# Where two weight pieces are rounded and split: in the attention by pairs, or in the memory steps behind it

## The chip, the cores and the metric

The kernel runs as one program on one core of a Trainium2 chip. The metric is the device time of one execution in microseconds. TensorE (PE) multiplies, VectorE (DVE) and ScalarE (ACT) work on its results, GpSimd (POOL) does a few side jobs, and SyncE (SP) issues the weight transfers.

## What is computed

The reference is two models in a row on 256 tokens of width 1024. The second one, "the second block" here, has two layers. Each of its layers mixes tokens with a windowed attention and a chunkwise matrix memory (an mLSTM), puts both results through one output projection, and then runs a feed-forward part (in the last layer a mixture of experts). Cut to what the change touches:

```
def merge_groups(att, h_ml, o_pre, g_att, g_ml, w_out):
    att_n = rmsnorm(att, g_att)
    hn = hf * lax.rsqrt(jnp.mean(hf * hf, axis=-1, keepdims=True) + EPS)      # hf: the memory's heads
    ml = hn.reshape(B, T, ML_WIDTH) * jax.nn.sigmoid(o_pre)
    return jnp.concatenate([att_n, ml], axis=-1) @ w_out

out_x = merge_groups(att_x, h_xf + flip(h_xb), om_x, g_att, g_ml, w_out)
out_c = merge_groups(att_c, h_cf + flip(h_cb), om_c, g_att, g_ml, w_out)      # first layer only
```

## The kernel before, in words

**Products of three.** A float32 product is made of three products in a rounded format. A weight piece of 128x2048 comes by DMA into a slot of `ring` (six slots). ScalarE rounds it into one of three slots of `ring_hi` (`weights_hi`, the copy at L1551), and VectorE subtracts the rounded part from the piece, in place (`weights_lo`, L2216, which writes `ring_r`). TensorE then reads both. `hi_upto(n)` and `lo_upto(n)` do the next roundings or subtractions until n pieces are done; `first_split["out0"]` and `first_split["out1"]` are the numbers of the first pieces of the two output projections, which have four pieces each. Because the engines run their instructions in the written order, the place of such a call in the code is its place in the engine's queue.

**Attention by pairs** (`attend_pairs(l)`, one for each engine, l is the layer, 0 or 1). A "half" is a pair of heads and 128 queries. There are 16 halves in the first layer (8 over 4x128 keys, 8 over 2x128 keys) and 8 in the last. For half n TensorE makes the scores, VectorE takes their maximum (L2281, L2283), ScalarE takes the exponential (L1630), TensorE turns it (L785), and VectorE and ScalarE each copy one head's turned part out of PSUM (into `pair_pT`, named `extra` in the profile). After every second half TensorE multiplies with the values, and VectorE evacuates that (L2304 to L2311). In this loop stand, in the kernel before, the roundings of pieces 0 and 1 (after n = 2 and 3, ScalarE) and their subtractions (after n = 3 and 5, VectorE).

**Memory steps.** They follow at once. A step n is one chunk, one memory head and one direction: 16 in the first layer, 8 in the last. A step's number n below is the loop index of this part. TensorE makes the row maximum and scores of step n+2 (`row_max`, L466) and then the step's product with the values, into bank 6 or 7 by turns (the rows with outputs of 128x129: 14 matmuls in the steps with four tiles). VectorE makes the exponents of step n+1 (L2785), the weights of step n (`weights`, L2801, which the product of step n waits for), and after each second step the scaled output of two steps (`heads_out`, L2816 to L2821). ScalarE makes the exponentials of step n+1 (L2000, L2002), which the weights of step n+1 wait for, and the magnitude of the step's denominator (L2033), and sums of squares (L2007, L2016). In the first layer, after step 4, ScalarE also takes a square root between two table loads (L1590, L1579). The bank of step n's product is free for step n+2 only when `heads_out` has read it.

**Output projection.** The heads are scaled and turned, rounded and split like the weights, and multiplied with the four pieces. Pieces 2 and 3 are rounded and split in this part, in both kernels.

Of the kernel before, what the change touches and what calls it, by code (L numbers as in the profile page):

```python
# [209 lines left out]
def build(nc, A, out):  # L210
    ctx = ExitStack()
    with ctx:
# [148 lines left out]
        first_split = {}  # L361
# [1185 lines left out]
        def _(act):  # L1547
# [64 lines left out]
            def attend_pairs(l):  # L1612
# [10 lines left out]
                for n, w in enumerate(hv):  # L1623
                    L.wait("pair_m", 16 * l + n + 1)
                    for hd in range(2):
                        if n >= 2:

                            look(act, "pair", l, "pT", n - 2, hd)
                        u, i = look(act, "pair", l, "s", n, hd), 2 * n + hd
                        leave(act.activation(pair_p[:, 2 * (n % 2) + hd, 0:w.keys * P], ps[:, u.bank, 0:w.keys * P],  # L1630
                                             ACT.Exp, bias=pair_neg[:, i:i + 1], scale=AD ** -0.5,
                                             accum_out=pair_den[:, i:i + 1]), u)
                    if n % 2:
                        j = n // 2
                        L.wait("pair_sink", 8 * l + j + 1)
                        v = pair_sink[:, 4 * j:4 * j + 4]
                        L.send(act.activation(v, v, ACT.Exp), "pair_esink")
                    if n:
                        copy_pT(n - 1)
                    if n in (2, 3):  # L1640
                        hi_upto(first_split[f"out{l}"] + n - 1)
                copy_pT(len(hv) - 1)

            def weights_hi(j):
# [299 lines left out]
            for l in range(2):  # L1944
# [81 lines left out]
                for n, (sq, x, d) in enumerate(steps):  # L2026
# [13 lines left out]
                        preload(ACT.Exp)  # L2040
                    if l == 0 and n in (6, 7):
                        mix_att((2 * n - 12, 2 * n - 11))
                    if l == 0 and n in MIX_AT:
                        mixT_hi(l, [MIX_AT.index(n)])
                    if n >= 2 and n % 2 == 0:
# [63 lines left out]
            with act.Fori(0, n_passes) as i:  # L2109
# [10 lines left out]
                for p, (e, c) in enumerate(EXPERT_ORDER):  # L2120
# [16 lines left out]
                    n = e * NP + c // 2  # L2137
# [15 lines left out]
        def _(dve):  # L2153
# [119 lines left out]
            def attend_pairs(l):  # L2273
# [47 lines left out]
                for n in range(len(hv)):  # L2321
# [4 lines left out]
                        heads(n // 2 - 1)  # L2326
                    if n >= 2 and n % 2 == 1:
                        output(n // 2 - 1)
                    if n in (3, 5):
                        lo_upto(first_split[f"out{l}"] + n // 2)  # L2330
                heads(len(hv) // 2 - 1)
                output(len(hv) // 2 - 1)

# [360 lines left out]
            for l in range(2):  # L2694
# [134 lines left out]
                for n in range(len(steps)):  # L2829
# [5 lines left out]
                    if l == 0 and n == 5:  # L2835
                        inverted("merge_rstd", 1, stat[:, 16:20])
                        dve.sem_inc(sig("merge_ready"), 1)
                    if l == 0 and n - 1 in MIX_AT:
                        mixT(l, [MIX_AT.index(n - 1)])
                heads_out(len(steps) // 2 - 1)  # L2840
# [271 lines left out]
```

## Time and profile before

| what | us |
|---|---|
| median of three runs | 2487.19 |
| lowest and highest | 2484.7, 2491.62 |
| the profiled execution | 2489.2 |
| its span, first to last instruction | 2487.4 |
| first layer: attention by pairs, then memory steps | about 885 to 937, then to 1008 |
| last layer: attention by pairs, then memory steps | about 1542 to 1578, then to 1617 |

The page has one line for each engine (busy time and share of the span), the span in 40 slices, the chain of work that ended last, and groups of instructions. TensorE is busy for 97% of the span, VectorE 68%, ScalarE 50%. The share of the whole span says nothing on the two places of the change, which together are about 160 us long; these are read from the rows in order of time. In such a row an idle time before an instruction stands in brackets, with what ended it; an idle time that is too short is left out, and rows that follow each other may overlap by what the pipeline overlaps.

### The profile page before, as it was taken

The numbers are of one execution on the slowest core, as the hardware profiler recorded it, in microseconds if no ns is written. First come the engines' busy times: TensorE is split into PE (matmuls) and PEld (weight loads), VectorE is DVE, ScalarE is ACT, GpSimd is POOL, SyncE is SP. The second block draws the span as 40 slices with busy tenths as digits, with TensorE's granted clock in tenths as the row PEclk, the third lists the DMA queues.
The fourth block names the chain that finished last, engine by engine and source line by source line (L and its number), as shares of the span: only waits on it lengthen the run. The fifth ranks groups of instructions, "written<-read, shape, count | busy, mean of one in ns | idle before, by whom it ended". The sixth has DMA issues, their size and how long they took to land.

```text
span 2487.4 us, 35121 instructions
## 1 busy us (share of the span) xinstructions
PE 2407.0 (97%) x13490; PEld 2008.3 (81%) x13514; DVE 1685.7 (68%) x1931; ACT 1233.3 (50%) x1471; POOL 436.4 (18%) x359
## 2 busy tenths in 40 slices
PE   8999999999999998899999999889999999999998
PEld 6669998879998866678888887578888888888887
DVE  7555864466854766467655348658888888888887
ACT  5454334444333354332222144447777777777775
POOL 1003541004520000010003500003122131121221
PEclk9999999999999998899999989989999999999999
DMA  6564554414552310135555332028989989989895
GB/s 237 213 244 163 187 187 148 150 60 154 186 196 87 105 43 1 48 121 188 201 196 185 127 107 97 1 88 313 369 333 353 357 333 363 347 339 370 332 363 208
DMA packets 71605, 503.59 MB, mean 202 GB/s; under 512 B 8208, under 2 KB 8720, under 8 KB 11536
## 3 DMA queue, kind: packets, MB, share of 16 engines
q1 hardware_dynamic: 70272, 496.68, 54.6%
q0 software_dynamic: 1168, 4.66, 0.5%
q8 instruction: 109, 1.79, 0.3%
q14 instruction: 56, 0.46, 0.1%
HBM read 500.26 MB, written 1.05 MB: 202 GB/s over the span
## 4 chain that ended last, share of the span: by engine, by line
PE 89%; DVE 5%; ACT 3%; issue 1%; POOL 1%; DMA 0%; SPq 0%; DVEq 0%; ACTq 0%
PE ps L466 85%; PE ps L530 1%; DVE h L2189 1%; POOL h_r L1433 1%; PE ps L1252 1%; DVE ring_r L2216 1%; DVE h_r L2183 1%; PE ps L785 1%; DVE temp L2281 0%; PE ps L634 0%; ACT ring_hi L1551 0%; DMA cols<-in_cols 0%; DVE temp L2552 0%; ACT h L1599 0%; DVE h L2801 0%
## 5 line engine op out<-in xcount | busy, mean ns | idle before, releaser
L1551 ACT ACTIVATE ring_hi<-ring 128x2048 fp32r<-128x2048 f32 x427 | 807.1, 1892 | 566.6 <-PE ps L466 345.4
L2988 DVE TENSOR_TENSOR ring_r<-ring,ring_hi 128x2048 fp32r<-128x2048 f32 x264 | 617.6, 2346 | 121.0 <-ACT ring_hi L1551 119.1
L466 PE MATMUL ps<-ring_hi,extra_r 128*128 128x512 f32 (+2 forms) x1808 | 607.9, 392 | 6.9 <-DVE ring_r L2216 4.8
L2216 DVE TENSOR_TENSOR ring_r<-ring,ring_hi 128x2048 fp32r<-128x2048 f32 (+3 forms) x163 | 380.3, 2340 | 180.2 <-ACT ring_hi L1551 166.2
L466 PE MATMUL ps<-extra_r,ring_hi 128*128 128x256 f32 (+1 forms) x1432 | 461.1, 322 | 8.4 <-DVE ring_r L2216 4.6
L466 PE MATMUL ps<-extra_r,ring_r 128*128 128x256 f32 (+1 forms) x1432 | 457.5, 319 | 0.0
L466 PE MATMUL ps<-h_r,ring_hi 128*128 128x256 f32 (+2 forms) x1400 | 445.1, 318 | 0.0
L466 PE MATMUL ps<-ring_r,extra_r 128*128 128x512 f32 (+2 forms) x1104 | 422.7, 383 | 0.0
L466 PEld LDWEIGHTS ps<-ring_hi,extra_r 128*128 128x128 f32 x1808 | 341.3, 189 | 80.5 <-DVE ring_r L2216 6.0
L466 PEld LDWEIGHTS ps<-extra_r,ring_hi 128*128 128x128 f32 x1432 | 273.4, 191 | 32.4 <-DVE ring_r L2216 5.2
L466 PEld LDWEIGHTS ps<-extra_r,ring_r 128*128 128x128 f32 x1432 | 273.3, 191 | 19.0
L466 PEld LDWEIGHTS ps<-h_r,ring_hi 128*128 128x128 f32 (+1 forms) x1400 | 267.6, 191 | 17.6
L466 PEld LDWEIGHTS ps<-ring_r,extra_r 128*128 128x128 f32 x1104 | 208.8, 189 | 37.9 <-issue 0.2
L1491 POOL TENSOR_TENSOR areaA_r<-areaA,ones 128x256 fp32r<-128x256 f32 x88 | 111.0, 1261 | 607.6 <-ACT areaA L2093 607.6
L466 PE MATMUL ps<-ring_hi,h_r 128*128 128x512 f32 (+2 forms) x400 | 147.2, 368 | 0.0
L466 PE MATMUL ps<-areaA_r,ring_hi 128*128 128x256 f32 (+1 forms) x736 | 140.8, 290 | 0.0
L466 PE MATMUL ps<-ring_hi,areaB_r 128*128 128x512 f32 x352 | 139.8, 397 | 0.0
L466 PE MATMUL ps<-ring_r,areaA_r 128*128 128x512 f32 x352 | 138.0, 392 | 0.0
L466 PE MATMUL ps<-ring_hi,areaA_r 128*128 128x512 f32 x352 | 137.7, 391 | 0.0
L466 PEld LDWEIGHTS ps<-areaA_r,ring_hi 128*128 128x128 f32 x736 | 117.0, 194 | 1.2
L1453 POOL TENSOR_TENSOR areaA_r<-areaB,areaA_r 128x256 fp32r<-128x256 f32 x44 | 115.8, 2633 | 3.5
L2552 DVE CUSTOM_DVE_ANT_0 temp<-ring,areaB 128x1024 f32<-128x1024 f32 x80 | 105.6, 1320 | 6.1 <-DVE areaA L2892 4.3
(372 smaller groups left out, 3014.0 us busy)
## 6 DMA issues: line engine op xcount, KB each, us to landing
ring<-in_experts SPq DMA_DIRECT2D x264, 1024.0 KB, 4.9
ring<-in_stream SPq DMA_DIRECT2D x202, 1024.0 KB, 4.9
ring<-in_stream SPq DMA_DIRECT2D x6, 512.0 KB, 3.7
ring<-in_stream SPq DMA_DIRECT2D x2, 576.0 KB, 3.6
res<-in_xT SPq DMA_DIRECT2D x2, 512.0 KB, 4.1
res<-in_ctxT POOLq DMA_DIRECT2D x1, 1024.0 KB, 7.3
h<-in_consts POOLq DMA_DIRECT2D x2, 512.0 KB, 5.1
areaB<-in_cond_rows POOLq DMA_DIRECT2D x1, 1024.0 KB, 6.3
```

The costliest lines, as they stand in the source:

```text
L466: return pe.matmul(o, l, r, start=start, stop=stop, skip_group_check=True)
L530: pe.matmul(ps[:, u.bank, :], warm_l, warm_r, start=True, stop=True, skip_group_check=True)
L785: m = pe.transpose(ps[:, u.bank, k * P:(k + 1) * P], pair_p[:, 2 * (n % 2) + hd, k * P:(k + 1) * P], ident)
L1252: m = pe.transpose(ps[:, 3, s * P:(s + 1) * P], mprod[:, n % 2, s * P:(s + 1) * P], ident)
L1433: pool.tensor_tensor(h_lo[:, hf, k, :], h[:, hf, k, :], h_hi[:, hf, k, :].bitcast(F32), ALU.subtract).then_inc(sig("h_lo"), 1)
L1453: pool.tensor_tensor(lo, src, hi.bitcast(F32), ALU.subtract).then_inc(sig("hidden_ready"), 1)
L1491: pool.tensor_tensor(hi, mturn[:, n % 2, :], ones[:, 0:1].broadcast_to([P, NM]), ALU.mult).then_inc(sig("moe_hi"), 1)
L1551: return act.activation(dst, src, ACT.Copy)
L2183: L.send(STT(out=h_lo[:, hf, k, :], in0=h[:, hf, k, :], scalar=shift(hf, k), in1=h_hi[:, hf, k, :].bitcast(F32), op0=ALU.add, op1=ALU.subt ...
L2216: L.send(TTN(ring_lo[:, s, 0:n], ring[:, s, 0:n], ring_hi[:, j % HIS, 0:n].bitcast(F32), ALU.subtract), "weights_lo")
L2552: S(dve.tensor_tensor_reduce(out=temp[:, :], in0=chunk[1][:, a * D:(a + 1) * D], in1=cond_rows[:, x, :], scale=1.0, scalar=0.0, op0=ALU.mu ...
L2988: TTN(ring_lo[:, s, :], ring[:, s, :], ring_hi[:, j % HIS, :].bitcast(F32), ALU.subtract).then_inc(sig("weights_lo"), 1)
```

## The change

The roundings of pieces 0 and 1 leave ScalarE's attention loop and stand in its memory loop: piece 0 in step 2, piece 1 in step 4, behind the sum of squares or the square root and ahead of L2016. The subtractions leave VectorE's attention loop and stand in its memory loop behind `heads_out`: piece 0 in step 4, piece 1 in step 6. This holds for both layers. The instructions themselves, their number, and the order on TensorE, GpSimd and SyncE stay as they are.

```diff
--- before.py
+++ after.py
@@ -1637,8 +1637,6 @@
                         L.send(act.activation(v, v, ACT.Exp), "pair_esink")
                     if n:
                         copy_pT(n - 1)
-                    if n in (2, 3):
-                        hi_upto(first_split[f"out{l}"] + n - 1)
                 copy_pT(len(hv) - 1)
 
             def weights_hi(j):
@@ -2040,6 +2038,8 @@
                         preload(ACT.Exp)
                     if l == 0 and n in (6, 7):
                         mix_att((2 * n - 12, 2 * n - 11))
+                    if n in (2, 4):
+                        hi_upto(first_split[f"out{l}"] + n // 2)
                     if l == 0 and n in MIX_AT:
                         mixT_hi(l, [MIX_AT.index(n)])
                     if n >= 2 and n % 2 == 0:
@@ -2326,8 +2326,6 @@
                         heads(n // 2 - 1)
                     if n >= 2 and n % 2 == 1:
                         output(n // 2 - 1)
-                    if n in (3, 5):
-                        lo_upto(first_split[f"out{l}"] + n // 2)
                 heads(len(hv) // 2 - 1)
                 output(len(hv) // 2 - 1)
 
@@ -2835,6 +2833,8 @@
                     if l == 0 and n == 5:
                         inverted("merge_rstd", 1, stat[:, 16:20])
                         dve.sem_inc(sig("merge_ready"), 1)
+                    if n in (4, 6):
+                        lo_upto(first_split[f"out{l}"] + n // 2 - 1)
                     if l == 0 and n - 1 in MIX_AT:
                         mixT(l, [MIX_AT.index(n - 1)])
                 heads_out(len(steps) // 2 - 1)
```

The line numbers of the kernel after are two lower from this loop on (L2016 is L2014 there, L2801 is L2799).

ScalarE in step 2 of the first layer, before: the denominator, two sums of squares, and the exponentials of step 4.

```order
L2033 ACTIVATE stat<-ps 128x2
L2007 ACTIVATE temp,stat<-areaA 128x512
L2016 ACTIVATE temp,stat<-areaA 128x128 x2
L2000 ACTIVATE h<-ps,temp 128x256 x2
L2002 ACTIVATE h<-h 128x512
```

After:

```order
L2031 ACTIVATE stat<-ps 128x2
L2005 ACTIVATE temp,stat<-areaA 128x512
L1551 ACTIVATE ring_hi<-ring 128x2048
L2014 ACTIVATE temp,stat<-areaA 128x128 x2
L1998 ACTIVATE h<-ps,temp 128x256 x2
L2000 ACTIVATE h<-h 128x512
```

One `ring_hi` instruction now stands between the first and the second sum of squares, ahead of the exponentials. Step 4 has the same, behind its last table load.

VectorE in step 4 of the first layer, before: `heads_out`, then the exponents of step 6 and the weights of step 5.

```order
L2816 TENSOR_TENSOR stat<-stat,temp 128x4
L2817 RECIPROCAL stat<-stat 128x4
L2819 TENSOR_TENSOR areaA<-ps,stat 128x2x128
L2821 SCALAR_TENSOR_TENSOR areaA<-ps,stat,areaA 128x128 x2
L2785 SCALAR_TENSOR_TENSOR h<-ps,temp,h 128x256 x2
L2801 SCALAR_TENSOR_TENSOR areaB<-ps,areaB 128x512 x2
```

After:

```order
L2814 TENSOR_TENSOR stat<-stat,temp 128x4
L2815 RECIPROCAL stat<-stat 128x4
L2817 TENSOR_TENSOR areaA<-ps,stat 128x2x128
L2819 SCALAR_TENSOR_TENSOR areaA<-ps,stat,areaA 128x128 x2
L2216 TENSOR_TENSOR ring_r<-ring,ring_hi 128x2048
L2783 SCALAR_TENSOR_TENSOR h<-ps,temp,h 128x256 x2
L2799 SCALAR_TENSOR_TENSOR areaB<-ps,areaB 128x512 x2
```

One `ring_r` instruction now stands ahead of those exponents and weights. Step 6 has the same.

VectorE behind half 3 of the first layer's attention, before: the maximum of half 5, an output, and the copy of half 4's turned part.

```order
L2281 TENSOR_REDUCE temp<-ps 128x2
L2283 SCALAR_TENSOR_TENSOR temp<-temp,rows 128x2
L2288 TENSOR_TENSOR temp<-temp,rows 128x4
L2311 TENSOR_TENSOR areaA<-ps,temp 128x2x128
L2216 TENSOR_TENSOR ring_r<-ring,ring_hi 128x2048
L2158 COPY extra<-ps 128x4x128
```

After:

```order
L2281 TENSOR_REDUCE temp<-ps 128x2
L2283 SCALAR_TENSOR_TENSOR temp<-temp,rows 128x2
L2288 TENSOR_TENSOR temp<-temp,rows 128x4
L2311 TENSOR_TENSOR areaA<-ps,temp 128x2x128
L2158 COPY extra<-ps 128x4x128
```

The subtraction ahead of the copy (`extra`) is gone; half 5 had the same.

## Rows read from the trace of the kernel before

**Rows 1.** The page: span, and the chain that ended last, by engine.

```profile
span 2487.4 us, 35121 instructions
...
PE 89%; DVE 5%; ACT 3%; issue 1%; POOL 1%; DMA 0%; SPq 0%; DVEq 0%; ACTq 0%
```

**Rows 2.** TensorE in order of time, first layer's attention: start, us, operation [idle <-releaser].

```profile
909.50 1.09 PE L785 MATMUL ps<-cst,h 128*128 128x128 f32 x8 [0.25 <-DVE extra L2158]
...
917.22 1.09 PE L785 MATMUL ps<-cst,h 128*128 128x128 f32 x8 [1.25 <-DVE extra L2158]
```

**Rows 3.** TensorE in order of time, last layer's attention.

```profile
1565.34 1.09 PE L785 MATMUL ps<-cst,h 128*128 128x128 f32 x8 [0.25 <-DVE extra L2158]
...
1573.06 1.09 PE L785 MATMUL ps<-cst,h 128*128 128x128 f32 x8 [1.89 <-DVE extra L2158]
```

**Rows 4.** VectorE in order of time, first layer's attention.

```profile
914.28 2.28 DVE L2216 TENSOR_TENSOR ring_r<-ring,ring_hi 128x2048 fp32r<-128x2048 f32 x1
916.48 0.68 DVE L2158 COPY extra<-ps 128x512 f32<-128x512 f32 x1
```

**Rows 5.** ScalarE in order of time, first layer's attention.

```profile
897.46 1.92 ACT L1551 ACTIVATE ring_hi<-ring 128x2048 fp32r<-128x2048 f32 x1
899.26 0.69 ACT L1630 ACTIVATE h<-ps,temp 128x512 f32<-128x512 f32 x1
```

**Rows 6.** Chain that ended last, first layer's memory steps: start, us, what.

```profile
959.34 0.69 ACT temp L2016 x4
...
961.31 1.29 DVE h L2801 x2
...
967.14 1.28 ACT L1579
...
970.72 1.29 DVE h L2801 x2
```

**Rows 7.** VectorE in order of time, first layer's memory steps.

```profile
964.68 1.28 DVE L2801 SCALAR_TENSOR_TENSOR areaB<-ps,areaB 128x512 f32<-128x512 f32 x2
...
974.10 1.28 DVE L2801 SCALAR_TENSOR_TENSOR areaB<-ps,areaB 128x512 f32<-128x512 f32 x2
```

**Rows 8.** TensorE in order of time, first layer's memory steps.

```profile
966.11 1.80 PE L466 MATMUL ps<-areaA,areaB 128*128 128x129 f32 x14 [0.26 <-DVE areaB L2801]
...
972.81 2.91 PE L466 MATMUL ps<-areaA,h 128*128 128x129 f32 x14 [1.38 <-DVE areaA L2819]
...
976.79 3.38 PE L466 MATMUL ps<-areaA,areaB 128*128 128x129 f32 x14
```

**Rows 9.** TensorE in order of time, last layer's memory steps.

```profile
1606.46 1.83 PE L466 MATMUL ps<-areaA,areaB 128*128 128x129 f32 x14
1610.06 1.83 PE L466 MATMUL ps<-areaA,h 128*128 128x129 f32 x14 [1.78 <-DVE areaA L2819]
1612.00 1.80 PE L466 MATMUL ps<-areaA,areaB 128*128 128x129 f32 x14
```

**Rows 10.** VectorE in order of time, last layer's memory steps.

```profile
1601.29 1.29 DVE L2801 SCALAR_TENSOR_TENSOR h<-ps,h 128x512 f32<-128x512 f32 x2 [0.54 <-ACT h L2002]
...
1604.97 1.28 DVE L2801 SCALAR_TENSOR_TENSOR areaB<-ps,areaB 128x512 f32<-128x512 f32 x2
```

**Rows 11.** Chain that ended last, last layer, behind the last memory step.

```profile
1614.24 0.18 ACT stat L2033
```

**Rows 12.** Busy us in stretches; the number after PEclk: is the granted clock's share.

```profile
core 0: us, PE busy (x) PEld busy (x) DVE busy (x) ACT busy (x) POOL busy (x), PEclk, DMA share, GB/s
976.00:980.00 4.00, 4.00 (x16) 3.22 (x15) 1.57 (x3) 2.24 (x7) 0.00 (x0) 0.50 0.02 4
1604.00:1608.00 4.00, 4.00 (x30) 3.47 (x30) 2.97 (x7) 2.00 (x8) 0.00 (x0) 1.00 0.00 0
```

**Rows 13.** TensorE in order of time, last layer, ahead of the first memory step.

```profile
1577.72 1.99 PE L466 MATMUL ps<-areaB 64*128 64x256 f32 x8
...
1580.70 3.59 PE L466 MATMUL ps<-areaB 64*128 64x256 f32 x8
```

## The prediction

> **What bounds the kernel now.** I read the page first: the span, and the chain that ended last by engine [rows 1]. 89% of that chain is TensorE, but the change leaves TensorE's own order alone, so the question is where TensorE waits. I therefore read TensorE in order of time at the two places of the change, and then the engine that is named in each bracket.
>
> In the attention by pairs TensorE is nearly always at work. Its idle times that have to do with the moved work are four: 0.25 and 1.25 us in the first layer [rows 2], 0.25 and 1.89 us in the last [rows 3]. Each ends with a copy into `extra` on VectorE, and that copy stands right behind a `ring_r` subtraction of 2.28 us, 2.20 us from start to start [rows 4]. The two roundings on ScalarE cost 1.80 us each from start to start [rows 5]; no idle time of TensorE follows them, because TensorE still has a half's scores or a product with the values to do.
>
> In the memory steps it is different. There the chain that ended last itself goes through ScalarE and VectorE: sums of squares of ScalarE in step 2, then (through exponentials) the weights of step 4 on VectorE at 961.31, and in step 4 the table load at 967.14, the same instructions again, and the weights of step 6 at 970.72 [rows 6]. The new place of piece 0's rounding is right ahead of the row at 959.34, that of piece 1's right behind the row at 967.14. Both are on the chain.
>
> **What is removed.** No instruction goes; four roundings and four subtractions (two of each per layer) change place. I take all four idle times as gained, since the copy that ends each moves forward by 2.20 us, more than any of them: 0.25 + 1.25 = 1.5 us in the first layer and 0.25 + 1.89 = 2.1 us in the last. Together 3.6 us. What is late next is TensorE itself. For the roundings that leave I count nothing. The bounds of this term are 0 (if another copy ends the same idle time) and 3.6; I stand by 3.6, because the rows show nothing else between the two instructions.
>
> **What is added, first layer.** Rounding piece 0: ScalarE's exponentials of step 4 come 1.80 us later, and the weights of step 4, which wait for them, too: 961.31 becomes 963.1. Everything behind is later by 1.80, as TensorE's product of step 4 waits for VectorE there. Rounding piece 1 is put between the table load and the sums, behind that product: another 1.80. The weights of step 6 go from 970.72 to 974.3, later by 3.6 us.
>
> Subtracting piece 0 (VectorE, step 4) adds 2.20 us ahead of the weights of step 5: from 964.68 [rows 7] to 964.68 + 1.80 + 2.20 = 968.7, so that TensorE's product of step 5 goes from 966.11 [rows 8] to about 970.0. It is over at 971.8. The weights of step 6 wait for ScalarE until 974.3 anyway, so this subtraction lies in the shadow of ScalarE and costs nothing of its own. If ScalarE's 3.6 us weren't there, it would cost up to 2.2.
>
> Subtracting piece 1 (VectorE, step 6) has no such cover. From the weights of step 6 to those of step 7 VectorE works without a break, 974.10 - 970.72 = 3.38 us [rows 6, 7]. With the subtraction it is 3.38 + 2.20 = 5.58 us, and the weights of step 7 run from 974.3 + 5.58 = 979.9 to 981.2. TensorE's product of step 7, which began at 976.79 [rows 8], begins at 981.2: later by 4.4 us. Of the 5.8 us by which the weights are late, 1.4 are absorbed by TensorE's own work between. Behind step 7 TensorE works through, so 4.4 us stay.
>
> **What is added, last layer.** The same with fewer covers. The weights of step 4 go from 1601.29 [rows 10] to 1603.1. From there to the weights of step 5 I take the 3.38 us of unbroken work plus 2.20: 1608.7 instead of 1604.97. They take 1.28, so TensorE's product of step 5 goes from 1606.46 [rows 9] to 1610.0, later by 3.5: here no square root hides the subtraction. The rounding of piece 1 on ScalarE runs beside it and is hidden. The product takes 1.83 us, to 1611.8; then ScalarE's magnitude and 1.4 us of `heads_out` to 1613.4, then the second subtraction to 1615.6, then the weights of step 7 to 1616.9, and TensorE's last product begins at 1617.0 instead of 1612.00 [rows 9]: 5.0 us. Before, the magnitude behind that product started at 1614.24 [rows 11], 0.4 us after the product's end, held by a table load; that slack is used up, and 4.6 us remain.
>
> Both additions have bounds. The lowest is 0, if the idle time of ScalarE and VectorE hid all; the highest is four roundings of 1.80 and four subtractions of 2.20, 16.0 us. The sum 4.4 + 4.6 = 9.0 us lies between and is worked out wait by wait, so I take it.
>
> **The clock.** In the first layer's memory steps the granted clock was 0.50 (1.2 GHz) from 976 to 980; in the last layer's it was 1.00 (2.4 GHz) from 1604 to 1608 [rows 12]. The fall in the first layer came behind 1.38 us of waiting, and the product of 14 matmuls then took 2.91 and 3.38 us in place of 1.83 [rows 8, 9]. The change puts waits of 1 to 2.4 us into both. In the first layer the product of step 7 is at the low level already, and could also meet the high one: 1.6 us to be lost or won. In the last layer that product would be 3.38 - 1.83 = 1.6 us longer if the clock has fallen by then. I take half of that, 0.8 us, as it lies between its two rows, and keep -1.6 and +5.4 (both layers, below) as the ends of the term.
>
> The Trainium skill, "TensorE: Matmul & The Clock Gate", section "HAM oscillation — how this bites in real kernels", says that gaps in a loop of matmuls throttle the clock again and that the penalty is paid at each return. By that rule the last layer's steps would lose the full level surely. The row of the first layer agrees with it; none of before shows it in the last layer. With the rule taken as certain the sum would be about 2 us higher; the sum here goes without it.
>
> **The sum.** -3.6 + 9.0 + 0.8 = +6.2 us. The profiled execution took 2489.2 us, so the same execution changed would take 2495.4. It was 2.0 above the median of 2487.2; against the median I predict 2493.4 us, 0.25% slower. About 0.3%, 7.5 us, is what a measurement can tell from no change, so "no change" here reaches up to 2494.7.
>
> **The rivals.**
> The clock falls in the last layer and comes back later in the first; this ends on the other side, slower by over 0.3%. For: the new waits, and the fall after 1.38 us [rows 8]. Against: in the last layer TensorE's product of step 6 waited 1.78 us and still took 1.83 us, and that of step 7 1.80 [rows 9]. Place: TensorE from step 5 on. Price: in the last layer the products of steps 5 and 7 are 1.1 (2.91 against 1.83) and 1.6 us longer, 2.7 in all, and I take the same again for the first layer, where two products behind step 7 would meet the low level. It decides once the clock takes 2.1 us (7.5 less 5.4). -3.6 + 9.0 + 2.7 + 2.7 = +10.8: 2498.0.
>
> The clock holds longer at the end of the attention. Ahead of the first memory step eight matmuls took 1.99 us at the high level and, a moment later, 3.59 at the low one [rows 13]. With the 1.89 us gone the fall might come later, or not at all: 1.6 us for these, as much again for what follows, some 3.5. Against: the first layer had only 1.25 us to wait, long before, and its clock fell there all the same. +5.4 - 3.5 + 0.8 = +2.7: 2489.9.
>
> The moved work hides. VectorE has idle time in the steps (0.54 us ahead of the weights of step 4, [rows 10]), and so has ScalarE; if the new instructions fall into such time, only the 3.6 us of gain are left: 2483.6, still within 0.3%. Against: the chain goes through just these places [rows 6]. With the clock held in both layers as well (another 7 us) it would be 2476.6, the one case that is faster by over 0.3%.
>
> **How the numbers follow.** My forecast (both effects, small clock term) 0.50; the clock falls 0.26; the clock holds 0.12; hidden 0.08; hidden and held 0.04. The forecast's own range, with a median that may lie 2 us off, is 2489 to 2497; 0.12 of its 0.50 lies above 2494.7. Slower by over 0.3% is then 0.26 + 0.12 = 0.38, within 0.3% is 0.38 + 0.12 + 0.08 = 0.58, faster 0.04. The range that leaves out 2 in 10 goes from 2487.5 (half of the hidden cases and some of the held below) to 2499.5 (the dearest of the clock cases above).
>
> **What would show it.** In the profile of the changed kernel: in the attention the idle times of 1.25 and 1.89 us before L785 are gone. The weights of step 4 begin some 1.8 us later than before, counted from the first product of the steps, those of step 6 by 3.6 in the first layer, and TensorE's product of step 7 by 4.4 and 5.0. New idle times of TensorE stand ahead of the products of steps 4 and 5, ended by VectorE. The attention of both layers is 1.5 and 2.1 us shorter, the memory steps some 4.5 longer each. The forecast is wrong if TensorE's new waits in the memory steps sum to less than the 3.6 us gained, or if the granted clock in the stretch between the attention's end and the first memory step is 1.00.

## The result, and the profile after

The kernel after took 2500.04 us, the median of 7 runs (2492.07 to 2505.79), beside 2487.19 for the kernel before (7 runs, 2484.7 to 2491.62). The ratio of the two is 1.0041, with an interval of 1.0029 to 1.0052; on 2487.2 that is 2497.4 us (2494.4 to 2500.1), slower by 10.2 us or 0.41%; the interval's lower end is 0.29%. Forecast were 2493.4 us and no change that can be told. The time is that of the first rival (2498.0), which had a chance of 0.26. The median of these seven runs lies 0.5 us above the range's upper end of 2499.5; what the ratio gives lies inside.

The runs of the kernel after spread over 14 us, those before over 7. The profiled execution is the fastest of the seven, 2492.07 us, and its span is only 2.9 us above that of before, so its trace holds less than a third of the loss. Its page, the line that answers to [rows 1]:

```profile
span 2490.3 us, 35145 instructions
```

TensorE in order of time, the first layer's attention and then the last layer's: the two places in each layer where before an idle time stood. The columns are those of [rows 2, 3].

```profile
909.26 1.09 PE L785 MATMUL ps<-cst,h 128*128 128x128 f32 x8
...
915.58 1.09 PE L785 MATMUL ps<-cst,h 128*128 128x128 f32 x8
```

```profile
1563.52 1.09 PE L785 MATMUL ps<-cst,h 128*128 128x128 f32 x8
...
1569.22 1.40 PE L785 MATMUL ps<-cst,h 128*128 128x128 f32 x8
```

No bracket is left in these rows: the idle times of 0.25, 1.25, 0.25 and 1.89 us that ended with `extra` are gone, all four, as forecast. One that wasn't forecast has come, 0.48 us ahead of the first layer's last turned half (931.95), ended by `extra` too.

The chain that ended last, first layer's memory steps, kernel after; it answers to [rows 6].

```profile
955.78 0.05 ACT ring_hi L1551
...
957.48 0.68 ACT temp L2014 x4
...
959.43 1.29 DVE h L2799 x2
...
961.03 0.43 DVE areaA L2817
...
961.51 3.39 PE ps L466 x14
...
964.93 0.17 ACT stat L2031
...
968.62 0.02 ACT ring_hi L1551
...
970.44 0.68 ACT temp L2014 x4
...
975.06 2.20 DVE ring_r L2216
```

Both roundings now stand on this chain (the rows at 955.78 and 968.62; ScalarE's next one starts 1.7 and 1.8 us later), and so does the second subtraction, at 975.06, ahead of the weights of step 7. The product of step 4 stands on it as well (961.51): ScalarE's magnitude of step 4 (964.93) waits for it, and the square root and the second rounding stand behind that. TensorE in the same steps of the kernel after, answering to [rows 8]: products of steps 4, 5, 6 and 7.

```profile
961.51 3.38 PE L466 MATMUL ps<-areaA,h 128*128 128x129 f32 x14 [1.37 <-DVE areaA L2817]
...
966.43 3.35 PE L466 MATMUL ps<-areaA,areaB 128*128 128x129 f32 x14 [0.39 <-DVE areaB L2799]
...
974.47 3.21 PE L466 MATMUL ps<-areaA,h 128*128 128x129 f32 x14 [1.37 <-DVE areaA L2817]
...
979.39 1.80 PE L466 MATMUL ps<-areaA,areaB 128*128 128x129 f32 x14 [1.09 <-DVE areaB L2799]
```

Two things can be read here. The products of steps 4 to 6 took 3.2 to 3.4 us and that of step 7 took 1.80; before, that of step 5 took 1.80, and those of steps 6 and 7 were the long ones [rows 8]: 14 matmuls take 1.8 us at the clock's high level (2.4 GHz) and 3.4 at the low one (1.2 GHz). And the product of step 7 now has a wait of its own, 1.09 us. The low level of step 4 costs time on the chain: the product of step 6 starts 28.05 us after the first product, and 26.39 in an execution of the same kernel (again_b below) whose step 4 took 1.83. The last layer's steps of the kernel after, products of steps 4 to 7, answering to [rows 9]:

```profile
1599.96 1.83 PE L466 MATMUL ps<-areaA,h 128*128 128x129 f32 x14 [1.03 <-DVE areaA L2817]
...
1604.88 2.85 PE L466 MATMUL ps<-areaA,areaB 128*128 128x129 f32 x14 [2.46 <-DVE areaB L2799]
1608.85 3.38 PE L466 MATMUL ps<-areaA,h 128*128 128x129 f32 x14 [1.13 <-DVE areaA L2817]
1612.99 1.80 PE L466 MATMUL ps<-areaA,areaB 128*128 128x129 f32 x14 [0.76 <-DVE areaB L2799]
```

Before, those of steps 5 to 7 took 1.83 us and less [rows 9]. Now the clock has fallen by the product behind the wait of 2.46 us. The granted clock in stretches of the kernel after, as in [rows 12]:

```profile
976.00:980.00 4.00, 2.91 (x16) 2.42 (x16) 3.88 (x7) 2.29 (x8) 0.00 (x0) 0.83 0.00 0
1604.00:1608.00 4.00, 2.85 (x14) 2.58 (x14) 2.87 (x7) 1.87 (x9) 0.00 (x0) 0.68 0.00 0
1608.00:1612.00 4.00, 3.15 (x14) 3.08 (x14) 3.90 (x7) 1.18 (x3) 0.00 (x0) 0.50 0.00 0
```

The first layer's stretch from 976 to 980 rose from 0.50 to 0.83, the last layer's from 1604 on fell from 1.00 to 0.68 and 0.50. These are stretches of the same times and not of the same instructions, because the first products start 3.6 and 4.9 us earlier in the kernel after (946.42 and 1585.59, before 950.00 and 1590.45); the rows of the products above compare like with like.

For all kernels below I cut the profiled execution at the same instructions. "Attention" runs from the first maximum of the scores (L2281) to the first product of the memory steps on TensorE, "steps" from there to VectorE's reciprocal of the heads' square root that stands ahead of the output projection (`stat`, 128x16 in the first layer, 128x20 in the last). "Step 7" is the time from that first product to the start of the product of step 7. The stretch between the two layers' parts has the same code in all kernels. Before, the four stretches of the two places sum to 194.6 us, more than the 160 given ahead of the prediction. All in us:

| kernel | span | attention 1 | steps 1 | step 7, first layer | between | attention 2 | steps 2 | step 7, last layer |
|---|---|---|---|---|---|---|---|---|
| before | 2487.4 | 63.26 | 58.42 | 26.79 | 536.06 | 45.97 | 26.95 | 21.55 |
| after | 2490.3 | 59.35 | 63.04 | 32.97 | 533.53 | 42.60 | 32.45 | 27.40 |
| again | 2495.7 | 58.42 | 63.17 | 33.12 | 536.18 | 42.52 | 34.45 | 27.84 |
| again_b | 2500.6 | 60.14 | 68.29 | 31.31 | 532.39 | 44.13 | 34.36 | 27.76 |
| again_c | 2491.6 | 60.11 | 62.75 | 31.33 | 536.35 | 42.54 | 33.01 | 27.96 |
| first_only | 2496.8 | 60.15 | 68.29 | 31.30 | 532.57 | 47.93 | 26.59 | 21.19 |
| last_only | 2491.7 | 60.44 | 58.42 | 26.80 | 536.05 | 42.44 | 34.76 | 28.15 |
| early | 2485.6 | 60.15 | 58.88 | 27.25 | 536.26 | 42.53 | 26.81 | 21.41 |
| lo_only | 2489.4 | 59.53 | 59.18 | 27.71 | 536.41 | 42.54 | 31.43 | 26.06 |
| hi_early | 2498.7 | 60.15 | 64.69 | 27.71 | 537.28 | 42.52 | 31.58 | 26.28 |
| warm | 2490.5 | 60.15 | 62.11 | 32.20 | 536.00 | 41.15 | 31.84 | 26.76 |
| step6_only | 2490.1 | 60.13 | 64.70 | 27.72 | 532.61 | 44.24 | 29.84 | 23.39 |
| early_warm | 2478.4 | 60.14 | 55.26 | 28.10 | 532.84 | 41.14 | 27.37 | 21.70 |

`after`, `again`, `again_b` and `again_c` are the same kernel. One execution against another differs by up to 5 us in stretches that the change doesn't touch ("between"), so single spans carry little; medians are used for the verdicts and this table for the places.

### The profile page after: what moved, and what is told of

It is laid out like the page before. It is cut to its first block, busy times and chain, and to the rows that moved or that the text cites. A ratio compares the mean times of both kernels' runs of the same rounds, so it can differ in the third digit from the quotient of the medians.

```text
span 2490.3 us, 35145 instructions
## 1 busy us (share of the span) xinstructions
PE 2413.4 (97%) x13514; PEld 2010.3 (81%) x13514; DVE 1688.9 (68%) x1931; ACT 1232.9 (50%) x1471; POOL 434.5 (17%) x359
## 4 chain that ended last, share of the span: by engine, by line
PE 90%; DVE 6%; ACT 2%; issue 1%; POOL 0%; DMA 0%; SPq 0%; DVEq 0%; ACTq 0%
PE ps L466 85%; PE ps L530 2%; DVE h L2189 1%; DVE ring_r L2216 1%; PE ps L1252 1%; PE ps L785 1%; DVE h_r L2183 1%; POOL h_r L1433 0%; PE ps L634 0%; DMA cols<-in_cols 0%; DVE temp L2550 0%; ACT ring_hi L1551 0%; ACT h L1599 0%; DVE h L2799 0%; DVE temp L2281 0%
```

## The experiments

Each edit is shown against the kernel after. The kernel before ran beside all of them, with medians of 2487.12 us (again, first_only, last_only, early), 2487.23 (lo_only, hi_early, warm, step6_only) and 2485.59 (again_b, again_c, early_warm).

**again: the kernel after, unaltered, five rounds.**

> The changed kernel once more, unaltered. Theory A (waits): the time is made in the two places of the change only. From the scores of the attention to the turned heads, the trace takes 0.7 us more in the first layer and 2.1 in the last, so the median is 2490 to 2492 and the executions at 2500 are made elsewhere. Rival B (clock): the two layers themselves differ between executions by where the granted clock falls; executions 8 us apart show it by a mean granted clock that is lower by about 0.004, and the median is 2497 to 2500 again.

Measured: 2497.29 us, ratio 1.0042 (1.0026 to 1.0057). The loss repeats, and with more runs the median stands at the value that the first ratio gave. The profiled execution's span was 2495.7 us, its steps of the last layer 34.45 us instead of 32.45: three products there took 3.20, 2.89 and 3.35 us, those of steps 4, 6 and 7. Of the two expectations, that of the clock fits (2497 to 2500); that of waits alone (2490 to 2492) doesn't. The granted clock of the whole execution goes with its time: of the 14 executions of this kernel in the two measurements, the six at 2500 us and above have 0.966 to 0.968, the eight below 0.968 to 0.973.

**first_only: the change in the first layer alone.**

```diff
+                    if l == 1 and n in (2, 3):
+                        hi_upto(first_split[f"out{l}"] + n - 1)
...
-                    if n in (2, 4):
+                    if l == 0 and n in (2, 4):
                         hi_upto(first_split[f"out{l}"] + n // 2)
...
-                    if n in (4, 6):
+                    if l == 0 and n in (4, 6):
                         lo_upto(first_split[f"out{l}"] + n // 2 - 1)
```

(The subtractions of the last layer stand in the attention again, after n = 3 and 5.)

> Only the first layer changed, the last as before. Theory A: +0.7 us against before (attention 3.9 shorter, memory steps 4.6 longer), within noise. Rival B: if the first layer's low stretch is what makes the executions at 2500, this one shows them too: +6 to +10 us in about half of the executions, and the last-layer-only kernel doesn't.

Measured: 2496.81 us, ratio 1.0033 (1.0021 to 1.0044), that is +8.2 us, where +0.7 was expected of the waits and +6 to +10 of the clock. The first layer costs most of the loss. The product of step 7 starts 31.30 us after the first product, before 26.79: 4.5 us are waits. With 1.5 us gained in the attention some 5 us are left, and the rows show the clock in their place. TensorE in order of time, first_only, steps 5, 6, 7 and 8:

```profile
968.71 3.04 PE L466 MATMUL ps<-areaA,areaB 128*128 128x129 f32 x14 [2.46 <-DVE areaB L2803]
...
975.20 2.79 PE L466 MATMUL ps<-areaA,h 128*128 128x129 f32 x14 [1.37 <-DVE areaA L2821]
...
980.11 3.35 PE L466 MATMUL ps<-areaA,areaB 128*128 128x129 f32 x14 [0.98 <-DVE areaB L2803]
...
987.45 1.50 PE L466 MATMUL ps<-areaA,h 128*128 128x129 f32 x6
```

Six matmuls took 1.50 us, where last_only, whose first layer is as before, shows:

```profile
979.71 0.83 PE L466 MATMUL ps<-areaA,h 128*128 128x129 f32 x6
...
981.60 0.83 PE L466 MATMUL ps<-areaA,areaB 128*128 128x129 f32 x6
```

In first_only the clock stayed low behind step 7, to the end of the steps: 68.29 us in all, against 62.75 to 63.17 in those executions of the same order in which it came back. From step 11 on the level is low in all of these, and in the kernel before too (its six matmuls of step 11, at 990.37, took 1.59 us), so what differs is steps 8 to 10 and the work beside them.

**last_only: the change in the last layer alone.** (The conditions the other way round: `l == 1` in the memory steps, `l == 0` in the attention.)

> Only the last layer changed, the first as before. Theory A: +2.1 us (attention 3.4 shorter, memory steps 5.5 longer). Rival B: if the clock that falls in the last layer's memory steps (product of step 5 at 2.85 us in place of 1.83) makes the executions at 2500, they are seen here, +6 to +10 us, and not with the first layer alone.

Measured: 2493.23 us, ratio 1.0018 (1.0009 to 1.0027), +4.5 us, between the two expectations (+2.1, and +6 to +10). The two layers alone sum to 12.7 us, against 10.4 for both at once; the intervals (5.2 to 10.9, 2.2 to 6.7, 6.5 to 14.2) allow that they just add up. The attention of the first layer, unchanged here, took 60.44 us and not the 63.26 of the profiled execution of before: that execution was a dear one in this stretch, and most of the 3.9 us by which the kernel after looks shorter there isn't the change's. With a low stretch of the same length behind the attention (about 7 us in all three) the kernel after and again are 1.1 and 2.0 us shorter than last_only; 1.5 was forecast.

**early: the four moved instructions earlier, into step 0 (ScalarE) and step 1 (VectorE).**

```diff
+                    if n == 0:
+                        hi_upto(first_split[f"out{l}"] + 2)
                     u = look(act, "lo", l, n)
...
-                    if n in (2, 4):
-                        hi_upto(first_split[f"out{l}"] + n // 2)
...
-                    if n in (4, 6):
-                        lo_upto(first_split[f"out{l}"] + n // 2 - 1)
+                    if n == 1:
+                        lo_upto(first_split[f"out{l}"] + 2)
```

> Both roundings in step 0 (behind the exponentials of step 1), both subtractions in step 1 (behind its weights), in both layers; there ScalarE waited 8.3 us and VectorE 4.8 and 5.7 us for TensorE in the kernel before. Theory A: the memory steps go back to their length of before (63.7 and 28.7 us) and the attention stays 3.9 and 3.4 us shorter: 7.3 us faster than before, 2480. At the least the 3.6 us of waits are gained: 2483.6. Rival B: the clock shift costs or gives another few us, to either side, so that the gain is not seen in the median: within 3 us of before.

Measured: 2483.60 us, ratio 0.9983 (0.9974 to 0.9992), -4.2 us. The expectation had 2480 with the attentions as short as in the profile of after, and 2483.6 "at the least"; the second came. This shows the first term of the prediction nearly by itself: with a hidden place for the work, leaving the attention is worth 3.6 us by the rows, and 2.0 to 6.5 by the runs. The steps of the last layer took 26.81 us (before 26.95), those of the first 58.88 (58.42).

**lo_only: only the subtractions moved; the roundings stay in the attention.**

```diff
+                    if n in (2, 3):
+                        hi_upto(first_split[f"out{l}"] + n - 1)
...
-                    if n in (2, 4):
-                        hi_upto(first_split[f"out{l}"] + n // 2)
```

> Only the subtractions moved (VectorE, memory steps 4 and 6); the roundings stay in the attention, as before. Theory A (waits worked out step by step): the attention is as short as in the changed kernel (42.5 us from the first score maximum to the first product in the last layer), the memory steps take about 59.4 us in the first layer (58.4 before, 63.1 changed) and 29.7 in the last (26.9 before, 32.5 changed). Sum against before about 0 to -2 us. Rival C: the roundings cost nothing in the memory steps and the subtractions all: 63 and 32.5 us, as in the changed kernel.

Measured: 2492.15 us, ratio 1.0020 (1.0010 to 1.0029), +5.0 us. Expected were 0 to -2 us, so this missed: the first layer's steps came out as worked out (59.18 us, expected 59.4), those of the last layer not (31.43, expected 29.7). There the product of step 5 took 3.26 us behind a wait of 1.76, and the product of step 7 waited 2.31. The four stretches of the two places account for 4.3 of some 9 us between this kernel and early; where the rest is made these single executions don't show. In the first layer the product of step 7 starts 0.9 us later than before, in the last layer 4.5. TensorE of lo_only in the first layer, steps 5 to 7:

```profile
964.65 1.80 PE L466 MATMUL ps<-areaA,areaB 128*128 128x129 f32 x14 [2.46 <-DVE areaB L2799]
...
969.15 2.45 PE L466 MATMUL ps<-areaA,h 128*128 128x129 f32 x14 [1.01 <-DVE areaA L2817]
...
974.06 3.21 PE L466 MATMUL ps<-areaA,areaB 128*128 128x129 f32 x14 [1.32 <-DVE areaB L2799]
```

The product of step 5 waits 2.46 us where it waited 0.26, and still took 1.80; the long products are behind it. That of step 6 starts 22.80 us after the first product, before 22.81: the subtraction of piece 0 lies in the shadow of the square root, as the prediction has it.

**hi_early: roundings in step 0, subtractions in steps 4 and 6 as in the kernel after.**

```diff
+                    if n == 0:
+                        hi_upto(first_split[f"out{l}"] + 2)
                     u = look(act, "lo", l, n)
...
-                    if n in (2, 4):
-                        hi_upto(first_split[f"out{l}"] + n // 2)
```

> The changed kernel with its two roundings in step 0, where ScalarE waits 8.3 us, in place of steps 2 and 4; subtractions in steps 4 and 6. Theory A: as with the roundings in the attention, 59.4 and 29.7 us of memory steps, so that the roundings' share of the loss is 3.6 and 2.8 us. Rival C: 63 and 32.5 us.

Measured: 2492.27 us, ratio 1.0023 (1.0014 to 1.0033), +5.7 us, the same as lo_only. So the roundings in steps 2 and 4 cost some 5 us, what this kernel lacks to the whole (with the two intervals, 0 to 9), and in step 0 about nothing. The lengths expected were 59.4 and 29.7 us; the profiled execution, the slowest of its runs, has 64.69 and 31.58. Its product of step 7 starts 27.71 us after the first, as in lo_only, and its first layer's steps are 5.5 us longer: the low level stayed to their end.

**warm: the kernel after, with small matmuls in TensorE's waits.** `keep_warm` issues matmuls of constants into the bank of the coming product, which overwrites them. They wait for nothing but that bank. Ahead of the products of steps 5 and 7, which wait for VectorE's weights, they stand in the wait; ahead of those of steps 4 and 6, which wait for the bank itself, they come behind it and delay the product.

```diff
                     u = take("lo", l, n, bank=6 + n % 2)
-                    if n == 0:
-                        keep_warm(u, 12)
+                    if n == 0 or n in (4, 5, 6, 7):
+                        keep_warm(u, 3 if n else 12)
```

> The changed kernel with three small bf16 matmuls more (as the kernel uses them elsewhere, results unused) on TensorE ahead of the products of steps 4 to 7 of both layers, where TensorE waits. Theory A: they fit into the waits of 0.4 to 2.5 us and change nothing: 2497. Rival B (the clock falls in the new waits): the products of steps 4 to 7 run at the high level, 1.8 us in place of 2.9 to 3.4, the first layer's memory steps stay at or under 63 us and the last's at or under 32.5, and the median falls by 3 to 8 us, with executions closer to each other.

Measured: 2492.18 us, ratio 1.0019 (1.0007 to 1.0031), against 1.0042 for the same kernel without them; 2497 was expected if they changed nothing, a fall of 3 to 8 us by the clock. TensorE in order of time, warm, last layer's steps 4 to 7:

```profile
1603.57 1.73 PE L466 MATMUL ps<-areaA,h 128*128 128x129 f32 x14
...
1607.73 1.83 PE L466 MATMUL ps<-areaA,areaB 128*128 128x129 f32 x14 [1.06 <-DVE areaB L2799]
...
1611.91 1.73 PE L466 MATMUL ps<-areaA,h 128*128 128x129 f32 x14
...
1615.30 1.83 PE L466 MATMUL ps<-areaA,areaB 128*128 128x129 f32 x14 [1.01 <-DVE areaB L2799]
```

All four products are at the high level, and the product of step 7 still starts 5.2 us later than before: waits without a fall of the clock, and some delay by the small matmuls themselves (the product of step 4 starts 15.03 us after the first, 14.37 in after). In the first layer only the product of step 6 is long (2.92 us). It starts 28.06 us after the first product, 1.67 later than in again_b: the small matmuls hold up the product of step 4 by 0.65 us and that of step 6 by 1.11. So warm has added work on the chain besides the waits.

**step6_only: roundings in step 0, the subtraction of piece 0 in step 1, that of piece 1 in step 6.**

```diff
+                    if n == 0:
+                        hi_upto(first_split[f"out{l}"] + 2)
...
-                    if n in (4, 6):
-                        lo_upto(first_split[f"out{l}"] + n // 2 - 1)
+                    if n in (1, 6):
+                        lo_upto(first_split[f"out{l}"] + 1 + n // 6)
```

> Roundings in step 0, first subtraction in step 1, second in step 6. Theory A: only the second subtraction costs: first layer +0.8 us (59.2), last layer +1.7 (28.6), so 2.5 us above the kernel with both in step 1, which had 0.9983 of before: about 2485.5. Rival C (one subtraction costs its full 2.2 us wherever it stands): +4.4, 2488.

Measured: 2486.33 us, ratio 1.0006 (0.9994 to 1.0018), against 0.9983 with both subtractions in step 1. One subtraction in step 6, two instructions in the whole program, moves the product of step 7 by 0.9 us in the first layer and 1.8 in the last, as the first expectation has it (0.8 and 1.7; the other had 2.2 for each). The 4.2 us are gone with it, by the ratios wholly, by the medians (2483.60 and 2486.33) for the greater part; the interval, 1.5 us below to 4.5 above before, hardly tells the expected 2485.5 and 2488 apart. The runs stand in two groups, six from 2484.7 to 2486.7 us and four from 2491.9 to 2494.2. The profiled execution (2491.89) is of the second group and shows the low level to the end of the first layer's steps (64.70 us).

**again_b and again_c: the kernel after in two more executions.**

> The changed kernel unaltered, one more profiled execution. Rival B as it stands after the kernel with the first layer alone (whose clock stayed at the low level from step 5 to the end of the first layer's steps, 68.3 us): an execution near 2500 has a stretch at the low level that does not end behind step 6 in the first layer, 66 to 69 us from the first product to the root of the sums; one near 2492 has 63. Theory A alone (fixed waits): 63 us whatever the execution's time.

> The same once more. Rival B: 66 to 69 us of first-layer memory steps or 34 to 35 in the last if the execution is near 2500, 63 and 32.5 if it is near 2492. Theory A alone: 63 and 32 us in either case.

Measured: 2502.41 and 2493.41 us. The granted clock in stretches, again_b and then again_c:

```profile
976.00:980.00 4.00, 3.19 (x14) 2.24 (x12) 4.00 (x6) 1.91 (x8) 0.00 (x0) 0.54 0.00 0
984.00:988.00 4.00, 4.00 (x12) 2.51 (x12) 2.44 (x8) 1.65 (x3) 0.00 (x0) 0.50 0.00 0
1000.00:1004.00 4.00, 4.00 (x12) 2.28 (x10) 2.08 (x7) 1.27 (x3) 0.00 (x0) 0.50 0.00 0
```

```profile
976.00:980.00 4.00, 2.77 (x11) 2.08 (x11) 3.39 (x7) 2.22 (x7) 0.00 (x0) 0.50 0.01 4
984.00:988.00 4.00, 3.73 (x20) 2.39 (x18) 3.07 (x8) 3.23 (x10) 0.00 (x0) 1.00 0.00 0
```

In again_b the clock stayed low to the end of the first layer's steps (68.29 us), in again_c it was back before 984 (62.75 us) and fell again between 988 and 992: 5.5 of the 9.0 us between the two executions lie in that one stretch. The rest lies elsewhere and partly cancels: again_b has 2.3 us more ahead of the first layer's attention, 4.0 less in "between", 2.9 more in the last layer's two stretches and 3.0 more behind them. The last layer's steps, 34.36 and 33.01 us, differ less than the expectation had it (34 to 35, and 32.5).

**early_warm: the early places, and four small matmuls ahead of the product of step 6.**

```diff
-                    if n == 0:
-                        keep_warm(u, 12)
+                    if n == 0 or n == 6:
+                        keep_warm(u, 4 if n else 12)
```

(On top of the edit of early.)

> The kernel with the early places, with four small bf16 matmuls more ahead of the product of step 6 in both layers, where TensorE waited 1.4 and 1.8 us. Rival B: in the first layer the product of step 6 and those behind it stay at the high level, its memory steps take 55 to 57 us in place of 58.9, and the median falls by 1 to 4 us under the early kernel (2483.6), to about 2481. Theory A alone: they fit into the waits and change nothing, 2483.6.

Measured: 2480.06 us, ratio 0.9978 (0.9969 to 0.9987), -5.5 us: the shortest of all, and faster than both kernels. TensorE in order of time, early_warm, first layer's steps 6 and 7:

```profile
973.32 3.07 PE L466 MATMUL ps<-areaA,h 128*128 128x129 f32 x14
...
976.95 1.83 PE L466 MATMUL ps<-areaA,areaB 128*128 128x129 f32 x14
```

The clock still fell (3.07 us; the expectation had step 6 at the high level), but the product of step 7 is at the high level (1.83), where it took 3.38 before. The steps took 55.26 us and not 58.42, as expected (55 to 57). Most of that comes later, though: the small matmuls delay the product of step 6 by 1.67 us against early, and step 8 starts only 0.3 us earlier than before. Six matmuls of step 11, the kernel before and then early_warm:

```profile
990.37 1.59 PE L466 MATMUL ps<-areaA,areaB 128*128 128x129 f32 x6 [0.95 <-DVE areaB L2801]
```

```profile
988.95 0.91 PE L466 MATMUL ps<-areaA,areaB 128*128 128x129 f32 x6 [0.94 <-DVE areaB L2799]
```

Behind nearly the same wait the level falls before and holds in early_warm, and by step 14 early_warm is 3.2 us ahead. Why it holds there isn't shown. That it beats early isn't shown either: the intervals overlap.

## Why the prediction was right or wrong, step by step

The forecast's range and sign held, and its steps up to the clock are borne out; the size, +10.2 us where +6.2 was worked out, failed in one term.

**The gain in the attention, -3.6 us.** Right. All four idle times are gone, and early, which has this term and nearly none of the others, measured -4.2. Some clock can come with it: in first_only, whose last attention is unchanged, the product with the values behind the waits of 1.89 and 0.52 us took 3.59 us; behind the same waits it took 1.95 before.

**The waits of the first layer, +4.4.** Right where the product of step 4 is at the high level: the product of step 7 starts 4.5 us later in first_only, again_b and again_c, and the weights of step 6 come 3.6 later in again_b (24.31 us after the first product, before 20.72), as worked out. In after and again it starts 6.2 and 6.3 us later. There the product of step 4 took 3.38 us, and the chain of after has it ahead of ScalarE's magnitude and rounding, so some 1.6 us of clock stand on the chain in a place where the prediction had none. It also falls as worked out: the subtraction of piece 0 is hidden by ScalarE's lateness (in lo_only by the square root), and that of piece 1 costs 0.9 alone (step6_only).

**The waits of the last layer, +4.6.** Right within what can be told. The product of step 7 starts 5.2 us later in warm, where no clock falls (5.0 forecast), and 5.9 to 6.4 in the four executions of the kernel after, where slow products lie ahead of it.

The two together: warm measured +4.7 us (0.0019 of 2487), and without the gain of 4.2 that early shows the steps cost 8.9; forecast were 9.0. That it meets so well is in part luck, because warm also has what its small matmuls delay (up to 1.7 us in the first layer) and one slow product.

**The clock, +0.8.** This is the step that failed, by its size. I wrote: "I take half of that, 0.8 us, as it lies between its two rows". Kernel after less warm is 1.0042 - 1.0019 = 0.0023, or 5.7 us, and the two measurements of the kernel after together leave about 2 to 9 (an estimate from the three intervals). As the small matmuls cost time too, the clock's share may be larger. The rival had 5.4. I reasoned about one product in each layer that may meet either level, and let a chance of one half stand for the size. The traces show more:
- In the last layer the clock falls in all five executions with all the new waits (those of the kernel after and last_only), and it takes two or three products along, not one (the product of step 7 itself took 1.80 us in after and again_c, 3.35 in the three others). The steps last 32.45 to 34.76 us, against 31.84 in warm with the same waits filled: 0.6 to 2.9 us.
- In the first layer the level either returns behind the product of step 7, or stays low to the end of the steps. The second costs 5.5 us more (68.29 against 62.75 in again_b and again_c, 64.69 against 59.18 in hi_early and lo_only, each pair with its product of step 7 at the same place). The rival's 2.7 us for this layer is neither of the two outcomes, so that its sum fits is partly luck. Of eight profiled executions with an idle wait ahead of that product, four kept the low level (first_only, again_b, hi_early, step6_only); of five without one (before, last_only, early, early_warm, warm), none. So few executions make that an association, not a proof; that small matmuls in the waits recover the time speaks for it too.

My argument against the rival, the last layer's product that waited 1.78 us and still took 1.83 [rows 9], was one row in which the clock outlasted a wait. The runs show a fall behind a shorter one, with no other wait in the 4 us ahead of it. The last layer of again_c, its granted clock and then the product of step 4:

```profile
1597.80:1601.80 4.00, 3.97 (x23) 2.94 (x22) 1.67 (x4) 4.00 (x12) 0.00 (x0) 1.00 0.00 0
```

```profile
1602.80 3.38 PE L466 MATMUL ps<-areaA,h 128*128 128x129 f32 x14 [1.03 <-DVE areaA L2817]
```

In four of the five executions with all the new waits the fall came already at this first one of 1.03 us; in after it came at the next, of 2.46. One row at the high level behind a wait doesn't say that the next such wait is safe. The Trainium skill tells of such falls under "TensorE: Matmul & The Clock Gate", "HAM oscillation — how this bites in real kernels": gaps that recur bring the throttle back, and each return is paid again. The waits of the kernel that it tells of are 3 to 5 us long; here waits of 1.03 to 2.46 us were enough, with products of 2.85 and 3.38 us behind them, so the measurement goes further than the section. I had counted that rule at about 2 us, and the first layer's stay at the low level is dearer than that.

**The profiled execution as the base.** It stood 2.0 us above its median, and I subtracted that as a whole, which was right: its first attention was some 2.8 us longer than the unchanged one of last_only, of which 1.7 are a longer stretch at the low level ahead of the first product (10.2 us against 6.8).

**The test that I named.** "The granted clock in the stretch between the attention's end and the first memory step" is 0.98 from 936 to 940 in the kernel after (0.90 before), in the last layer it falls as before but a few matmuls later. Over the 18 us ahead of the first product of the steps, read in stretches of 1 us, the last layer's low level lasts over 10 us in both executions whose attention is unchanged (before, first_only) and in two of the eleven others (again_b, step6_only); in the other nine it lasts 7 us or less. In the first layer both lengths occur with the change and without it. So the rival of the held clock is partly true in the last layer. Its size can't be told from single executions: the last layer's attention took 45.97 and 47.93 us where it is unchanged (before, first_only) and 42.4 to 44.2 where the work has left it (warm and early_warm 41.1), and 2.1 of that are the waits.

Still open is what decides, from one execution to the next, whether the low level ends behind step 7. Again_b and again_c have the same waits ahead of it (2.46, 1.37 and 1.2 us), and I found nothing in their rows ahead of the return that tells them apart. Open too is why in the first layer the clock falls at step 4 in after and again and at step 5 in the other two, behind the same wait of 1.37 us ahead of step 4.

## What to carry to other kernels

A wait of one or two microseconds put into a stretch where TensorE already waits can be priced twice: once as the wait, once as the matmuls behind it at half the clock; here 9 us of waits brought some 6 us of clock, with an interval of about 2 to 9. When work moves from one place to another, look for a place where the engine is ahead of its reader (here steps 0 and 1; in steps 2, 4 and 6 the same instructions were on the chain), and where a wait can't be avoided, try a few small matmuls in it. They belong ahead of a product that waits for its operand: where it waits for its bank they come behind the wait and are paid for. Read several executions before pricing a clock effect: of this kernel one profiled execution shows less than a third of the loss and another more than all of it.

## What the runs showed of the hardware

- The granted clock can stay at its low level for over 25 us while TensorE is nearly always at work: in again_b from the product of step 7 (980.3) to the end of the first layer's steps, with 0.50 in the stretches shown and TensorE busy for all 4.00 us of them. In again_c the same instructions had 1.00 from 984 to 988, and 0.50 again from 992 on. The low level from there to the end of the steps is in the kernel before too.
- The same kernel's executions differ with the clock that they were granted: 2492.07, 2492.51 and 2494.53 us at 0.971 to 0.973, and 2500.04 to 2505.79 at 0.966 to 0.968. The stretch of 5.5 us is one cause; of the slower four of these seven no trace was taken, so that it is theirs isn't shown.
- A wait of 1.03 us of TensorE, behind 4 us in which it was busy for 3.97 at a granted clock of 1.00, was followed by 14 matmuls at the low level (3.38 us, again_c); a wait of 1.78 us in the kernel before was followed by 14 at the high level (1.83).
- Small matmuls of constants at four products of each layer gave back about half of the 10 us (ratio 1.0042 to 1.0019), though they brought none of these products' operands sooner and delayed some products by 0.4 to 1.1 us.
